# Two stacked transformer blocks on one core: moving the split weights of the MLPs' second product by 128 bytes in SBUF, and memory's keys and values by 32

## The reference, cut to what matters

```python
def cross_attention(h, mem_n, wq, wkv, wo):
    q = (h @ wq).reshape(B, S, X_HEADS, X_HEAD_DIM)
    kv = (mem_n @ wkv).reshape(B, M, 2, X_HEADS, X_HEAD_DIM)
    ...
def sq_relu_mlp(h, w1, w2):          # w1: 1024 x 4096, w2: 4096 x 1024
    a = jax.nn.relu(h @ w1)
    return (a * a) @ w2
```

## The kernel before, in words

| tensor | role in the large products | place before | place after |
|---|---|---|---|
| whi, wlo, MH, ML, P0, P1, YH, Tb, PTb | both | 0 | 0 |
| PSH, PSL; E3, E3R | moving; in cross attention E3R is stationary too | -64 | -64 |
| PRH, PRL | moving | -32 | -32 |
| MEMH, MEML | both | 192 | 192 |
| WMH, WML | stationary, second product of the MLPs | 96 | -32 |
| KT, KTR (memory's keys) | moving | 0 | -32 |
| VM, VMR (memory's values) | stationary | 0 | -32 |

## Time and profile before

### The profile page before, as it was taken

How to read it: one execution, slowest core, us unless ns; L and a number is a source line. 1 busy time by engine, 2 the same in 40 slices (tenths; PEclk the granted TensorE clock), 3 DMA queues, 4 the chain that set the end, 5 groups by cost and what they waited for, 6 DMA issues and landing times.

```text
span 2178.4 us, 32363 instructions
## 1 busy us (share of the span) xinstructions
PE 2165.3 (99%) x12328; PEld 1856.0 (85%) x12328; DVE 1495.4 (69%) x2518; ACT 998.9 (46%) x1724; POOL 14.5 (1%) x14
## 2 busy tenths in 40 slices
PE   9999999999999999999999999999999999999998
PEld 8887888888788888888898888888888888888887
DVE  5866665557656567686666777766887658777775
ACT  5445543434445344375554544443434435444444
POOL 0000000000000000200000000000000000000000
PEclk9999999999999999999999999999999999999999
DMA  5655543345645333464364233333233313333331
GB/s 199 184 178 162 154 128 108 105 130 179 190 137 151 121 104 115 139 179 151 112 168 127 87 109 98 104 99 105 88 98 106 96 39 107 97 97 107 100 111 51
DMA packets 136698, 268.19 MB, mean 123 GB/s; under 512 B 21773, under 2 KB 79931, under 8 KB 136160
## 3 DMA queue, kind: packets, MB, share of 16 engines
q1 hardware_dynamic: 136544, 266.13, 40.0%
HBM read 235.37 MB, written 26.77 MB: 120 GB/s over the span
## 4 chain that ended last, share of the span: by engine, by line
PE 99%; DVE 0%; DMA 0%; ACT 0%; issue 0%; DVEq 0%; SPq 0%; ACTq 0%
PE ps L2349 31%; PE ps L2351 30%; PE ps L2350 30%; PE ps L2366 2%; PE ps L2377 2%; PE ps L2401 0%; PE ps L2403 0%; PE ps L2391 0%; PE ps L2390 0%; PE ps L2402 0%; PE ps L2389 0%; PE ps L2420 0%; DMA t_X<-in_xT 0%; PE ps L2426 0%; DVE t_X L3107 0%
## 5 line engine op out<-in xcount | busy, mean ns | idle before, releaser
L2349 PE MATMUL ps<-t_P0H,t_whi 128*128 128x512 f32 (+1 forms) x1072 | 418.9, 391 | 1.7 <-DVE t_P0L L2713 1.7
L2350 PE MATMUL ps<-t_P0L,t_whi 128*128 128x512 f32 (+1 forms) x1072 | 413.1, 385 | 0.0
L2351 PE MATMUL ps<-t_P0H,t_wlo 128*128 128x512 f32 (+1 forms) x1044 | 403.3, 386 | 0.0
L2668 DVE TENSOR_TENSOR t_wlo<-t_raw,t_whi 128x1024 fp32r<-128x1024 f32 (+1 forms) x262 | 309.2, 1182 | 40.6 <-PE ps L2351 29.2
L2492 ACT ACTIVATE t_whi<-t_raw 128x1024 fp32r<-128x1024 f32 (+1 forms) x267 | 270.9, 1021 | 83.9 <-PE ps L2351 82.4
L2349 PEld LDWEIGHTS ps<-t_P0H,t_whi 128*128 128x128 f32 x1072 | 201.6, 188 | 54.6 <-issue 14.1
L2350 PEld LDWEIGHTS ps<-t_P0L,t_whi 128*128 128x128 f32 x1072 | 201.8, 188 | 39.4 <-issue 1.0
L2351 PEld LDWEIGHTS ps<-t_P0H,t_wlo 128*128 128x128 f32 x1044 | 196.5, 188 | 40.2
L2499 ACT ACTIVATE t_whi<-t_raw 128x1024 fp32r<-128x1024 f32 x90 | 94.9, 1057 | 152.3 <-DVE t_raw L2683 145.7
L2350 PE MATMUL ps<-t_PRL,t_WMH 128*128 128x512 f32 x416 | 164.3, 395 | 0.0
L2351 PE MATMUL ps<-t_PRH,t_WML 128*128 128x512 f32 x416 | 164.3, 395 | 0.0
(11 more groups left out here) (383 smaller groups left out, 4775.1 us busy)
## 6 DMA issues: line engine op xcount, KB each, us to landing
t_raw<-in_wts SPq DMA_DIRECT2D x362, 512.0 KB, 3.6
far<-t_Tb SPq DMA_DIRECT2D x26, 384.0 KB, 3.2
far<-t_Tb SPq DMA_DIRECT2D x16, 512.0 KB, 3.7
t_PTX<-far SPq DMA_DIRECT2D x64, 96.0 KB, 3.5
t_raw<-in_wts SPq DMA_DIRECT2D x16, 384.0 KB, 3.2
t_QKV<-far SPq DMA_DIRECT2D x32, 128.0 KB, 3.0
t_raw<-in_wts SPq DMA_DIRECT2D x13, 256.0 KB, 3.0
t_PTX<-far SPq DMA_DIRECT2D x24, 128.0 KB, 2.9
```

The source lines that it names most:

```text
L2349: e.matmul(s.out, s.sh, s.mh, start=s.first, stop=False, skip_group_check=again)
L2350: e.matmul(s.out, s.sh, s.ml, start=False, stop=False, skip_group_check=again)
L2351: i = e.matmul(s.out, s.sl, s.mh, start=False, stop=s.end, skip_group_check=again)
L2668: e.tensor_tensor(s.dst, s.raw, s.hi.bitcast(F32), ALU.subtract).then_inc(*mark("lo", s.j))
```

## The change

`WMH`/`WML` start 128 bytes lower, from 96 above the place of `MH` to 32 below it. To make room, `KT` and `VM`, which lie between `E3` and `MH`, start 32 bytes lower too. (`oh`, `frow`, `rel` and `lvec`, small tables that share the memory of KT, move with it.) Nothing else moves, the total size is the same, and no instruction, wait or order is changed.

```diff
-SHIFT_P1, SHIFT_M = 32, 96
+SHIFT_P1 = 32
...
     put("E3R", [128, 16, 512], F32R, put("E3", [128, 16, 512], offset=second - SHIFT_E3))
-    at[0] += 16 * 512 * 4
+    at[0] += 16 * 512 * 4 - SHIFT_P1
     T["SQ2"] = T["E3"][:, 14, :]
     kt = put("KT", [128, 8, 256])
...
     put("lvec", [128, 256], offset=kt + 5184)
+    put("WML", [128, 8, 256], F32R, put("WMH", [128, 8, 256], F32R, at[0]) + 8192)
+    at[0] += SHIFT_P1
     put("MH", [128, 8, 256], F32R)
     put("ML", [128, 8, 256], F32R)
     put("MEML", [128, 8, 256], F32R, put("MEMH", [128, 8, 256], F32R, at[0] - 16384 + SHIFT_MEM) + 8192)
-    put("WML", [128, 8, 256], F32R, put("WMH", [128, 8, 256], F32R, at[0] - 16384 + SHIFT_M) + 8192)
     at[0] += SHIFT_MEM
```

## The result

The changed kernel took 2184.31 us in the median of 13 runs (2183.81 to 2186.30), against 2179.52 for the kernel before (13 runs). The ratio is 1.0023, with a 95% interval of 1.0014 to 1.0031: 4.8 us slower, where 8.6 us faster was forecast. The profiled execution had a span of 2183.2 us, against 2178.4.

The account below looks back on a forecast made before the run. The prediction took PE, busy throughout the MLPs at full clock, as the bound. WM products -8.2 us and entries -0.4 us gave -8.6, from 2179.45 to 2170.9 us; own range 2169 to 2175, 8-in-10 range 2162 to 2180.5.

Parts of the forecast that it names:

- What bounds the kernel: Both MLP stretches: PE always busy at full clock, nothing else near; the change acts only through the distance between matmul starts.
- The steady distance of the WM products: 1248 WM products in the MLPs: equal places make them 6.6 ns cheaper each, 8.2 us less.
- The entries: 104 entries into WM groups, where a WM block loads during a 256-wide matmul: 4 ns each, 0.4 us less.
- What stays as it is: P1, PS and PR with whi: costs must stay unchanged, since their places don't change.
- KTR and VMR: 64 matmuls moving KTR and 64 with VMR stationary, 256 wide: taken as 0, bounds 0.6 us either way.
- The sum: Whole kernel: -8.2 - 0.4 = -8.6 us, giving 2170.9 us from the median 2179.45.
- The moving operand alone: Rival for 512-wide matmuls: only the moving place sets cost, WM products stay at 233.3 ns; 2179.0 us, chance 0.32.
- The observation that spoke for it: P0 moving at place 0 while E3R at -64 is loaded: next matmul still comes after 0.22 us.
- The collision: Rival: both streams at equal places disturb each other, WM products cost 4 to 5 ns more; 2185.1 us, chance 0.16.
- The deeper gain of 220 ns: Rival: WM products at the new pair cost 220 ns, below any 512-wide form seen; 2162.5 us, chance 0.10.
- The Trainium skill's rule on two independent read ports: Weight loads take no read bandwidth from the running matmul, so the time would stay 2179.45 us.

Follow-up runs that it names:

- the program of turns: Matmuls only, no kernel: 12 of 512 columns at one pair of places, then 24 of 256 at -64 and 0, five turns without pause; changed kernel's pair 5.607 us a turn.
- E3R: Not a run but a buffer: operand of 256-wide matmuls; E3R by whi went from 277 to 281 ns in the changed kernel.
- the table of differences: Matmul-only program, stretches of 24 after a pause, sorted by stationary less moving place modulo 256; 512 columns 227 to 234 ns.
- -32 and 160: Kernel before with WMH and WML at place 160 instead of 96, PR still at -32: 2174.24 us, ratio 0.9976.
- 0 and 192: Kernel before with PR at place 0 and WM at 192: 2172.54 us, ratio 0.9969.
- program of stretches after a pause: First part of a matmul-only program: stretches of 24 at given moving and stationary places, each after a pause of about 1 us; 256 columns moving at -64, 113 to 120 ns.

## Why the prediction was wrong, point by point

*What bounds the kernel.* Right. PE stayed busy through both MLPs, DVE and ACT stayed far off, and the writes of WML took 1218 ns as in the earlier trace rows. Only the distances between matmuls changed.

*The steady distance of the WM products.* Right in sign, wrong in size: the forecast was 6.6 ns each, 8.2 us less; measured were 233.3 to 231.6 ns, 2.1 us less. So 6.1 us of the miss lie in this term. The reading behind it was right as far as it went. The difference of the two places decides, and a difference of 0 does cost 227 ns in a long stretch at -32 and -32 too. But inside groups of 12 behind 256-wide matmuls that pair doesn't come to this rate: in the program of turns it has 231.6, where 0 and 0 has 226.7 and -64 and -64 228.9. The prediction took the price at 0 and 0 for that of every equal pair, in a long stretch as in a short one. At a difference of 128, the old pair's, a stretch after a pause has mostly 232.

*The entries.* Right in sign and size. The last 256-wide matmul ahead of a group went from 123 to 120 ns, 0.3 us over 104 entries, where 0.4 was forecast. The 3.39 us more of the 256-wide matmuls hold it already.

*What stays as it is.* This is the step that failed, and that turned the sign. The prediction says that P1 with whi, PS with whi and PR with whi "must stay as they are, since their places don't change". It costed the change only where operands moved, and took each form's row as a property of its places. For PS and E3R with whi (and with the buffers Tb and PTb that stand in for it) it is not: 2136 matmuls in the two MLPs went from about 114.6 to 117.8 ns, 6.8 us, because another pair of places ran ahead of them. The prediction has this term at nothing. The trace of before held the sign of it. Near 1593 us, E3R by whi ran 24 matmuls from 1593.65 to 1596.47, 117.5 ns each, behind P0 by ML, both at place 0, where stretches of 24 behind the WM groups took 114.6. The grouped row of E3R by whi, 360 matmuls with a mean of 277, had averaged this away.

```profile
1593.65 0.28 PE L2349 MATMUL ps<-t_E3R,t_whi 128*128 128x256 f32 x1
...
1596.47 0.39 PE L2349 MATMUL ps<-t_P0H,t_MH 128*128 128x512 f32 x1
```

*KTR and VMR.* Taken as 0 with bounds of 0.6 us; KTR cost 0.3 us more, and the experiment that moved only these showed no difference that can be measured.

*The sum.* Forecast was 8.6 us less, measured 4.8 more, 13.4 apart. Of this the WM products account for 6.1 us, the 256-wide matmuls behind them for 7.2 (6.8 more instead of 0.4 less), and the cross attentions for 0.4. The 0.3 us by which these exceed 13.4 lie within what executions of one kernel differ by.

*The rivals.* The moving operand alone: refuted by the table of differences, where 0 and 0 and -64 and -64 are equally cheap. For this kernel's groups it was the nearer price even so: the 12 took 2.78 us, nearer to its 2.80 than to the 2.72 of the forecast. The observation that spoke for it, concerns a difference of 192, which the table has at 229, nearly as cheap as 0. The collision, forecast at 2185.1 us, hit the time by luck (2184.3 measured): its cause was not at work, for the WM products did not get dearer. The deeper gain of 220 ns does not exist in any of the 64 pairs of 512 columns. The Trainium skill's rule on two independent read ports ("TensorE: Matmul & The Clock Gate", section "Step-by-step: what each phase is for") does not hold to the nanosecond here: 512-wide triples cost 227 to 234 ns by the difference of places. Whether the load takes read bandwidth from the matmul or they meet in another way no run shows.

*What stays open.* Why a rate persists, and what chooses it. The runs show two rates for a stretch of 256 columns with a difference of 64, each kept to its end. Behind the pairs of the kernel before and of the changed one the rate was the same every time without a pause. Behind -64 and 0, behind -32 and 160 and behind 11 pairs of the program of turns it was not, and after a pause either came. The runs do not show what holds it.

## What to carry to other kernels

When PE is the bound, a buffer's place shifts the cost of the matmuls that read it and also of those that run right behind them, so cost a layout by the whole turn of streams, not by the instructions whose operands move. A grouped row is a mean over histories; look in the timeline for the same form behind another neighbour before using it as a price. A bare program of the matmuls in their real order, run once, told which layouts to try, which the trace could not, and a one-line edit from its table gave 8 us. It is not exact: -32 and 160 has the shorter turn in it than 0 and 192, but in the kernel the longer MLPs (265.3 to 265.6 us against 264.9). For some pairs its rate depends on what ran earlier, and -32 and 160, steady in it from turn to turn, had both rates in the kernel. So measure the kernel itself.

## What the runs showed of the hardware that was not expected

- The distance of consecutive matmuls with weight loads depends on stationary place less moving place, modulo 256 bytes: with 512 columns 227 ns at 0, 229 at 192, 232 to 234 else; with 256 columns 113 at 64 and 116 to 120 else, but for one stretch at 192 that took 113 (program of stretches after a pause).
- The 256-wide stream at a difference of 64 has two rates, about 113.5 and 117.8 ns. In the kernels all 102 stretches behind -32 and 96 took the first and all 102 behind -32 and -32 the second. But behind -64 and 0 one program had six fast turns of six and the other only slow ones, and behind 0 and 128 the rate changed from turn to turn.
- Equal places cost 226.7 ns in groups of 12 at 0 and 0, 231.6 at -32 and -32 and 228.9 at -64 and -64, between the same 256-wide stretches: there the absolute place, or its distance to the neighbours' places, enters too.
